# Two heads side by side and six score slots in a stick-breaking attention stage

## What is computed

```python
z = jnp.einsum('bhqd,bhkd->bhqk', q, k) * scale          # scale = 64 ** -0.5
mask = key_pos[None, :] < q_pos[:, None]
log_keep = jnp.where(mask, jax.nn.log_sigmoid(-z), 0.0)
suffix = lax.cumsum(log_keep, axis=3, reverse=True) - log_keep
a = jnp.where(mask, jnp.exp(jax.nn.log_sigmoid(z) + suffix), 0.0)
out = jnp.einsum('bhqk,bhkd->bhqd', a, v)
```

## Time and profile before

| | us |
|---|---|
| median of three runs | 5630.05 |
| lowest, highest | 5625.33, 5639.29 |
| the profiled execution, its own time | 5640.03 |
| its span from first to last instruction | 5637.9 |
| PE matmul busy | 4779.1 (85%) |
| PE weight loads busy | 3883.8 (69%) |
| DVE, ACT, POOL busy | 2049.0 (36%), 1568.2 (28%), 147.0 (3%) |
| mean granted clock of PE | 0.905 of full speed |

### The profile page before, as it was taken

One profiled execution on the slowest core, in us unless ns is written; L12 is line 12 of the kernel. 1 busy time (PEld: TensorE's weight loads), 2 busy tenths in 40 slices (PEclk: granted clock), 3 DMA queues, 4 the chain that ended last, 5 costly groups with the idle time before them and its releaser, 6 DMA issues. The chain is left out here.

```text
span 5637.9 us, 78328 instructions
## 1 busy us (share of the span) xinstructions
PE 4779.1 (85%) x29460; PEld 3883.8 (69%) x29460; DVE 2049.0 (36%) x3521; ACT 1568.2 (28%) x2832; POOL 147.0 (3%) x125
## 2 busy tenths in 40 slices
PE   5968887976987886678699889999977968899998
PEld 4957787954966875566553368888765757688886
DVE  2536641444224554232224333332233135323333
ACT  1441122233232122222235522222233223222221
POOL 0000000022000000000012200000000000000000
PEclk7989898988977988889899989999988979999998
DMA  2111111111210000301100011111110121111111
GB/s 74 45 32 52 35 32 46 45 51 55 67 38 19 13 13 29 115 24 41 31 28 15 8 38 49 49 48 49 38 42 25 40 60 40 36 48 48 48 48 57
DMA packets 380807, 235.68 MB, mean 42 GB/s; under 512 B 28803, under 2 KB 361891, under 8 KB 380597
## 3 DMA queue, kind: packets, MB, share of 16 engines
q1 hardware_dynamic: 380596, 232.75, 14.3%
HBM read 174.83 MB, written 24.02 MB: 35 GB/s over the span
## 5 line engine op out<-in xcount | busy, mean ns | idle before, releaser
L2001 PE MATMUL ffp_acc<-ff_m_hi_rounded,ffp_w_hi_rounded 128*128 128x512 f32 x1024 | 400.4, 391 | 25.6 <-DVE ff_m_rounded L2046 25.6
L2001 PE MATMUL ffp_acc<-ff_m_hi_rounded,ffp_w_rounded 128*128 128x512 f32 x1024 | 400.0, 391 | 0.0
L2001 PE MATMUL ffp_acc<-ff_m_rounded,ffp_w_hi_rounded 128*128 128x512 f32 x1024 | 399.9, 391 | 0.0
L2001 PE MATMUL ffp_acc<-ff_inner_hi_rounded,ffp_w_hi_rounded 128*128 128x512 f32 x1024 | 398.3, 389 | 0.0
L2001 PE MATMUL ffp_acc<-ff_inner_hi_rounded,ffp_w_rounded 128*128 128x512 f32 x1024 | 398.3, 389 | 0.0
L2001 PE MATMUL ffp_acc<-ff_inner_rounded,ffp_w_hi_rounded 128*128 128x512 f32 x1024 | 398.3, 389 | 0.0
L2012 ACT ACTIVATE ffp_w_hi_rounded<-ffp_w 128x256 fp32r<-128x256 f32 x512 | 190.5, 409 | 567.4 <-DMA ffp_w<-w_mlp_dram 279.7
L2042 DVE TENSOR_TENSOR ffp_w_rounded<-ffp_w,ffp_w_hi_rounded 128x256 fp32r<-128x256 f32 x512 | 199.0, 422 | 124.7 <-ACT ffp_w_hi_rounded L2012 117.0
L2001 PEld LDWEIGHTS ffp_acc<-ff_m_hi_rounded,ffp_w_hi_rounded 128*128 128x128 f32 x1024 | 193.3, 189 | 67.4 <-issue 27.2
L2001 PEld LDWEIGHTS ffp_acc<-ff_m_rounded,ffp_w_hi_rounded 128*128 128x128 f32 x1024 | 193.2, 189 | 40.4
L2001 PEld LDWEIGHTS ffp_acc<-ff_m_hi_rounded,ffp_w_rounded 128*128 128x128 f32 x1024 | 193.3, 189 | 40.2
(11 more groups left out here) (645 smaller groups left out, 10930.4 us busy)
## 6 DMA issues: line engine op xcount, KB each, us to landing
ffp_w<-w_mlp_dram SPq DMA_DIRECT2D x256, 128.0 KB, 2.2
ffp_w<-w_up_dram SPq DMA_DIRECT2D x128, 128.0 KB, 2.2
ffp_w<-w_down_dram SPq DMA_DIRECT2D x128, 128.0 KB, 2.2
delta_stage<-b_pool SPq DMA_DIRECT2D x9, 1152.0 KB, 6.1
pa_w<-w_in_dram SPq DMA_DIRECT2D x72, 128.0 KB, 2.5
pb_w<-w_in_dram SPq DMA_DIRECT2D x68, 128.0 KB, 2.5
b1o_mix<-mix SPq DMA_DIRECT2D x2, 4096.0 KB
p1o_w<-w_out_dram SPq DMA_DIRECT2D x64, 128.0 KB, 2.2
```

Of the source, the lines that this page charges most:

```text
L2001: mm = nc.tensor.matmul(acc[s][:, c, :], rounded(a[:, s, k, :]), rounded(b[:, k, at]), start=(k == 0 and i == 0), stop=(k == KD - 1 and i ...
```

## The change

The scores contract over 64 rows: `q` is one [P, SEQ] buffer without zeros, and head e multiplies partitions 64e to 64e + 63 of `k` and `q`. `scores` and `apply` work on a step (both heads) instead of a unit, the two heads' products one behind the other; `apply` waits for both heads first. PE's order in step p is `scores(p + 2)`, the sums of both heads, `apply(p - 1)`. ACT and DVE go by steps too. There are six slots. `out` is [P, 2, 512], both heads of a chunk in one bank; it is cleared by two products of 128*128, after the scores of steps 0 and 1. The memset of `qz` is gone; scaling of q and the copy of `out` are one instruction each. POOL's code is unchanged.

```diff
--- before.py
+++ after.py
@@ -1702,7 +1702,7 @@
 
     PAIRS, QC = HEADS2 // 2, SEQ // 512
     units = [(qc, kt, e) for qc in range(QC) for kt in range(4 * qc + 3, -1, -1) for e in range(2)]
-    U, SL = len(units), 4
+    U, SL = len(units), 6
 
     def span(u):
 
@@ -1718,13 +1718,13 @@
         mat = lambda n: mt[:, names.index(n), :]
         k = part.sb("k", [P, SEQ])
         vs = part.sb("vs", [P, NT, P])
-        qz = part.sb("qz", [P, 2, SEQ])
+        q = part.sb("q", [P, SEQ])
         ex, soft, att = (part.sb(n, [P, SL, 512]) for n in ("ex", "soft", "att"))
         run = part.sb("run", [P, 2, 512])
         score = part.ps("score", [P, SL, 512])
-        out = part.ps("out", [P, 4, 512])
+        out = part.ps("out", [P, QC, 512])
         S = {n: part.sem(n) for n in (
-            "loaded", "staged", "stage_used", "zeroed", "q_ready", "z_done", "absd", "expd", "logd", "soft_done",
+            "loaded", "staged", "stage_used", "q_ready", "z_done", "absd", "expd", "logd", "soft_done",
             "summed", "weighed", "masked", "run_done", "applied", "out_read", "d")}
         block = part.stack.enter_context(nc.Block())
         n_diag = sum(span(u)[1] for u in range(U))
@@ -1742,35 +1742,17 @@
             M = nc.tensor.matmul
             pe.wait_ge(S["loaded"], 16 * len(names))
             with pe.Fori(0, PAIRS) as i:
-                def scores(u):
-                    qc, kt, e = units[u]
-                    o, _ = span(u)
-                    if u >= SL:
-                        pe.wait_ge(S["weighed"], i * U + u - SL + 1)
-                    M(score[:, u % SL, o:], k[:, kt * P:(kt + 1) * P], qz[:, e, qc * 512 + o:(qc + 1) * 512],
-                      start=True, stop=True).then_inc(S["z_done"], 1)
-                pe.wait_ge(S["staged"], i * 32 + 32)
-                pe.wait_ge(S["q_ready"], i + 1)
-                pe.wait_ge(S["out_read"], i + 1)
-                for e in range(2):
-                    for qc in range(QC):
-                        M(out[64 * e:64 * e + 64, 2 * e + qc, :], mat("zeros")[:, 0:64], qz[:, e, qc * 512:(qc + 1) * 512],
-                          start=True, stop=True)
-                scores(0)
-                scores(1)
-
-                def apply(u):
-                    qc, kt, e = units[u]
-                    o, _ = span(u)
-                    if span(u)[1]:
-                        pe.wait_ge(S["masked"], i * n_diag + sum(span(w)[1] for w in range(u + 1)))
-                    else:
-                        pe.wait_ge(S["weighed"], i * U + u + 1)
-                    M(out[64 * e:64 * e + 64, 2 * e + qc, o:], vs[:, kt, 64 * e:64 * e + 64], att[:, u % SL, o:],
-                      start=False, stop=True, skip_group_check=True).then_inc(S["applied"], 1)
-                for u in range(U):
-                    if u + 2 < U:
-                        scores(u + 2)
+                def scores(p):
+                    for u in (2 * p, 2 * p + 1):
+                        qc, kt, e = units[u]
+                        o, _ = span(u)
+                        half = slice(64 * e, 64 * e + 64)
+                        if u >= SL:
+                            pe.wait_ge(S["weighed"], i * U + u - SL + 1)
+                        M(score[:, u % SL, o:], k[half, kt * P:(kt + 1) * P], q[half, qc * 512 + o:(qc + 1) * 512],
+                          start=True, stop=True).then_inc(S["z_done"], 1)
+
+                def sums(u):
                     o, _ = span(u)
                     pe.wait_ge(S["soft_done"], i * U + u + 1)
                     mm = M(score[:, u % SL, o:], mat("neg_from"), soft[:, u % SL, o:], start=False, stop=True,
@@ -1780,9 +1762,33 @@
                         mm = M(score[:, u % SL, o:], mat("neg_ones"), run[:, units[u][2], o:], start=False, stop=True,
                                skip_group_check=True)
                     mm.then_inc(S["summed"], 1)
-                    if u >= 1:
-                        apply(u - 1)
-                apply(U - 1)
+
+                def apply(p):
+                    for u in (2 * p, 2 * p + 1):
+                        if span(u)[1]:
+                            pe.wait_ge(S["masked"], i * n_diag + sum(span(w)[1] for w in range(u + 1)))
+                        else:
+                            pe.wait_ge(S["weighed"], i * U + u + 1)
+                    for u in (2 * p, 2 * p + 1):
+                        qc, kt, e = units[u]
+                        o, _ = span(u)
+                        M(out[64 * e:64 * e + 64, qc, o:], vs[:, kt, 64 * e:64 * e + 64], att[:, u % SL, o:],
+                          start=False, stop=True, skip_group_check=True).then_inc(S["applied"], 1)
+                pe.wait_ge(S["staged"], i * 32 + 32)
+                pe.wait_ge(S["q_ready"], i + 1)
+                scores(0)
+                scores(1)
+                pe.wait_ge(S["out_read"], i + 1)
+                for qc in range(QC):
+                    M(out[:, qc, :], mat("zeros"), q[:, qc * 512:(qc + 1) * 512], start=True, stop=True)
+                for p in range(U // 2):
+                    if p + 2 < U // 2:
+                        scores(p + 2)
+                    sums(2 * p)
+                    sums(2 * p + 1)
+                    if p >= 1:
+                        apply(p - 1)
+                apply(U // 2 - 1)
 
         @block.scalar
         def _(act):
@@ -1808,10 +1814,13 @@
                         act.wait_ge(S["applied"], i * U + u - SL + 1)
                     A(att[:, u % SL, o:], score[:, u % SL, o:], ACT.Exp).then_inc(S["weighed"], 1)
                 softplus(0)
-                for u in range(U):
-                    if u + 1 < U:
-                        softplus(u + 1)
+                softplus(1)
+                for u in range(0, U, 2):
+                    for w in (u + 2, u + 3):
+                        if w < U:
+                            softplus(w)
                     weigh(u)
+                    weigh(u + 1)
 
         @block.gpsimd
         def _(pool):
@@ -1834,16 +1843,11 @@
         @block.vector
         def _(dve):
             V, T = nc.vector, nc.vector.tensor_tensor
-            V.memset(qz[:, :, :], 0.0).then_inc(S["zeroed"], 1)
-            dve.wait_ge(S["zeroed"], 1)
             dve.wait_ge(S["loaded"], 16 * len(names))
             dve.sem_inc(S["stage_used"], 1)
             dve.sem_inc(S["out_read"], 1)
             with dve.Fori(0, PAIRS) as i:
-                for e in range(2):
-                    half = slice(64 * e, 64 * e + 64)
-                    q = V.tensor_scalar(qz[half, e, :], qk[half, bass.ds(i, 1), :].rearrange("p a n -> p (a n)"), 0.125, None, ALU.mult)
-                q.then_inc(S["q_ready"], 1)
+                V.tensor_scalar(q[:, :], qk[:, bass.ds(i, 1), :].rearrange("p a n -> p (a n)"), 0.125, None, ALU.mult).then_inc(S["q_ready"], 1)
 
                 def soft_of(u):
                     o, diag = span(u)
@@ -1863,16 +1867,15 @@
                         a = att[:, u % SL, o:o + P]
                         T(a, a, mat("before"), ALU.mult).then_inc(S["masked"], 1)
                 soft_of(0)
-                for u in range(U):
-                    if u + 1 < U:
-                        soft_of(u + 1)
+                soft_of(1)
+                for u in range(0, U, 2):
+                    for w in (u + 2, u + 3):
+                        if w < U:
+                            soft_of(w)
                     mask_of(u)
+                    mask_of(u + 1)
                 dve.wait_ge(S["applied"], i * U + U)
-                for e in range(2):
-                    half = slice(64 * e, 64 * e + 64)
-                    c = V.tensor_copy(dst[half, bass.ds(i + 4, 1), :].rearrange("p a (q n) -> p (a q) n", n=512),
-                                      out[half, 2 * e:2 * e + 2, :])
-                c.then_inc(S["out_read"], 1)
+                V.tensor_copy(dst[:, bass.ds(i + 4, 1), :].rearrange("p a (q n) -> p (a q) n", n=512), out[:, :, :]).then_inc(S["out_read"], 1)
                 dve.sem_inc(S["stage_used"], 1)
```

## The result

The changed kernel takes 5559.3 us in the median of four runs (5553.9 to 5563.0) against 5628.3 for the kernel before; the ratio is 0.9873, with a 95% interval of 0.9856 to 0.9890. The prediction was 5561 us, in 5542 to 5592. The profiled execution took 5557.8 us, its span is 5556.1.

What follows compares the result with a forecast made beforehand. PE was taken as the bound, ACT next. Per round -15.3 - 2.0 - 1.9 + 2.2 gives 17.0 us less; four rounds 68 plus 1.2 for the last copy, 69 us: 5561 us in the median, range 5542 to 5592.

Steps and rivals of the forecast that it cites:

- Streaming: PE's matmul columns in a round: paired scores and paired applies share one time, 284 to 212 blocks, -15.3 us.
- The rival of half the packing: Scores do not overlap, or pass order spoils both pairs: 42 us gained in all, 5588 us, chance 0.17.
- Turns: PE's changes of tile form: 0.55 us in each of 12 steps, 6.6 us a round against 8.6, -2.0 us.
- Opening: Start of a round, scores now before the zero products: 4.1 us against 6.0, -1.9 us a round.
- waits for ACT: PE waiting at scores and sums of a round's first seven steps: +2.2 us a round, bounds 0 and 4.
- Close: End of a round: copy and query scaling stay inside the 5.5 us transfer; -1.2 us once, behind the last round.
- full packing: Main case, both scores and both applies of a step side by side: 5561 us, alone 5542 to 5573, chance 0.70.
- The clock: Rival: 1.2 GHz lasts beyond the opening, up to 50 us lost a round; 5661 us at half the round, chance 0.04.

## Why the prediction was right

**Streaming, -15.3 us a round: right.** It rested on two tiles at once. Applies had a row of their own kind; scores did not, and took the value of the nearest rows. The full step with only the scores undone grew by 0.66 us, with only the applies undone by 1.19, and with both to the old 7.55. The rival of half the packing (5588 us) asked for a full step of 6.6; it is 5.70.

The Trainium skill (TensorE: Matmul & The Clock Gate, section Part 3: Packing small matmuls — row/col tiling) has matmuls start strictly in order. By that rule the pairs would take three pass times each, 0.43 us more than they do. The changed kernel's score passes start in twos, 7 ns apart, both heads' first ones together, so this case does not agree with it.

**Turns, 0.55 us a step: right** (0.58 in a full step). The one with no row, from 64*128 to 128*128, was put at 0.20 us. Scores to sum take 1.06 us (2923.35 to 2924.41), less the 0.854 of streaming: 0.21.

**Opening and waits for ACT: the sum about right, the parts less so.** The prediction had 4.1 us for the opening and 2.2 of waits. In a round of 57.3 us, streaming is 45.3, turns 6.5 (ten steps at 0.58, two without scores at 0.37) and the opening 4.0 (the product behind the zeros starts 4.7 us after the round, 4.6 without its turn, and 0.6 of this is streaming); 1.5 us are left for the waits. In rounds 2 and 4 the late clock adds 1.05. The mean round is 57.8 us, 58.2 was forecast. That ACT decides the narrow steps was right as a mechanism: one ACT call less in three took 0.54 us off the stretch with the largest wait and nothing off a full step. The largest wait of the prediction's tally, 0.8 us at the scores of step 5, is 0.6: 4.59 us between the first sums of steps 2 and 3, less 16 blocks of 0.2135 us and 0.58 of turns. The others are 1.0 us together where 1.4 was put.

**Close: right, with one thing overlooked.** The last copy is 1.23 us for 2.46, once. The pause also shrank from 5.5 to 5.3 us each time.

**The sum.** 4 x 17.25 us of rounds (75.1 to 57.8 in the mean), 0.7 of the three pauses, 1.2 at the end: 70.9 us against 69. The upper bound of full packing alone was added up a little too high: turns 0.6 and waits 1.8 us above the forecast in four rounds give 5571 us, not 5573. The range does not rest on it.

**The clock.** I gave this rival 0.04, and in the changed kernel it did not come: 1.00 through all full steps. But its mechanism is real in this stage. A second fall came along with more waiting in the narrow steps in three experiments: in every round with half the rows unpaired, in three of four with four slots, in two of four with Abs twice. In the changed kernel PE is busy for 3.86 of 4 us behind the first rise, and the clock stays:

```profile
2893.00:2897.00 4.00, 3.86 (x18) 2.48 (x16) 1.81 (x6) 3.14 (x8) 2.01 (x5) 1.00 0.02 4
```

That the fuller steps are the reason was not tried by itself, and why the same instructions keep the clock in one round and lose it in another stays open.

## What to carry to other kernels

Two small products cost one when they stand directly behind each other, use different rows or different columns of the array, and all that both wait for is waited for ahead of the first; half a tile with no partner saves nothing and costs a turn, here 0.2 us a unit. Once the bound engine has lost a quarter of its work, look at the steps in which the next engine is the slower one, and give them slots to run ahead: they were worth 33 us here, nearly all of it in the narrow steps. And a pause of the bound engine for a transfer costs twice, in itself and in the clock of the next microseconds: a second buffer each for `k`, `q` and `vs` took 22 us off this stage, 16 of them the pauses themselves.

## What the runs showed of the hardware that was not expected

- Two 64*128 tiles that write the same 128 PSUM partitions in two banks run side by side with no loss to be seen: 1.06 us for four passes of 512 columns and the turn behind them.
- The clock can fall to 1.2 GHz again in the middle of a round behind waits of PE that look harmless: 1.35 of 2 us busy in one case, one wait of 2.05 us in the second, one of 1.47 us (1.83 of 3.3 us busy) in the third. In the last two kernels it does so in some rounds only, though all run the same instructions.
- When it rises varies from round to round for the same instructions: 4.1 or 6.3 us after the start of the changed kernel's rounds, with 3.14 or 3.71 us for the same four zero passes and the first sum at 5.5 or 6.6 us. In one first round, with PE busy all the time, it rose only after 8.9 us.
- Records of loads name the last semaphore they passed as releaser even if it had been given 0.3 us before; the end of the named instruction has to be compared with the start of the wait.
